# Ten stages of a float32r transformer kernel: the moving halves at ten offsets instead of one

## The reference, cut to what matters

```python
def swiglu(h, w_gate_up, w_down):
    gate, up = jnp.split(h @ w_gate_up, 2, axis=-1)
    return (jax.nn.silu(gate) * up) @ w_down
```

## Time and profile before

| what | value |
|---|---|
| median of 2 runs | 1613.93 us (1613.84 to 1614.02) |
| the profiled execution | 1613.48 us |
| its span, first to last instruction | 1611.7 us |
| PE busy | 1577.5 us, 98% |
| PEld busy | 1418.1 us, 88% |
| DVE busy | 991.0 us, 61% |
| ACT busy | 825.9 us, 51% |
| mean granted TensorE clock | 0.995 |

### The profile page before, as it was taken

How to read it: one execution, slowest core, us unless ns; L and a number is a source line. 1 busy time by engine, 2 the same in 40 slices (tenths; PEclk the granted TensorE clock), 3 DMA queues, 4 the chain that set the end, 5 groups by cost and what they waited for, 6 DMA issues and landing times.

```text
span 1611.7 us, 25494 instructions
## 1 busy us (share of the span) xinstructions
PE 1577.5 (98%) x10721; PEld 1418.1 (88%) x10721; DVE 991.0 (61%) x1661; ACT 825.9 (51%) x1191; POOL 153.2 (10%) x141
## 2 busy tenths in 40 slices
PE   7999999999999999999999999999999999989997
PEld 6878899987889989998899999889888888879986
DVE  6786744445645575556665667668747776665554
ACT  4565543444569755444454465444544546354442
POOL 2220010100002200111001100001000000001100
PEclk9999999999999999999999999999999999999999
DMA  9757866777663356556555576598572565585552
GB/s 332 249 178 252 274 219 229 246 247 245 237 211 105 111 194 200 190 192 218 192 183 178 189 148 193 182 187 175 135 156 62 143 158 182 167 265 190 195 190 78
DMA packets 224417, 309.40 MB, mean 192 GB/s; under 512 B 5004, under 2 KB 146720, under 8 KB 224304
## 3 DMA queue, kind: packets, MB, share of 16 engines
q1 hardware_dynamic: 222208, 301.48, 61.1%
q0 software_dynamic: 1664, 5.84, 1.0%
q10 hardware_dynamic: 432, 0.45, 0.1%
HBM read 306.71 MB, written 1.05 MB: 191 GB/s over the span
## 4 chain that ended last, share of the span: by engine, by line
PE 86%; DVE 8%; ACT 4%; issue 1%; DMA 1%; POOL 0%; ACTq 0%; DVEq 0%
PE ps L137 84%; PE ps L140 2%; DVE wl L150 2%; DVE SM L160 1%; DVE MT L160 1%; ACT wh L146 1%; ACT L146 1%; ACT SA L146 1%; DVE X L160 0%; ACT SA L147 0%; DMA raw<-in_a_w_qkv_dram 0%; DVE MT L157 0%; DMA X<-in_x_dram 0%; ACT FT L146 0%; DVE SM L157 0%
## 5 line engine op out<-in xcount | busy, mean ns | idle before, releaser
L150 DVE TENSOR_TENSOR wl<-raw,wh 128x1024 fp32r<-128x1024 f32 x498 | 611.6, 1267 | 395.8 <-ACT wh L146 395.1
L146 ACT ACTIVATE wh<-raw 128x1024 fp32r<-128x1024 f32 x498 | 502.0, 1053 | 228.5 <-PE ps L137 109.1
L137 PE MATMUL ps<-XPf,wh 128*128 128x256 f32 x1408 | 243.5, 279 | 0.0
L137 PEld LDWEIGHTS ps<-XPf,wh 128*128 128x128 f32 x1408 | 212.8, 188 | 4.5 <-ACT wh L146 2.5
L137 PE MATMUL ps<-XPf,wl 128*128 128x256 f32 x704 | 195.5, 278 | 0.0
L137 PE MATMUL ps<-XPc,wh 128*128 128x256 f32 x832 | 145.8, 280 | 0.0
L137 PE MATMUL ps<-wh,HTH 128*128 128x512 f32 x352 | 137.6, 391 | 0.0
L137 PE MATMUL ps<-wl,HTH 128*128 128x512 f32 x352 | 137.2, 390 | 0.0
L137 PE MATMUL ps<-wh,HTL 128*128 128x512 f32 x352 | 137.2, 390 | 0.0
L137 PEld LDWEIGHTS ps<-XPf,wl 128*128 128x128 f32 x704 | 132.9, 189 | 0.0
L137 PEld LDWEIGHTS ps<-XPc,wh 128*128 128x128 f32 x832 | 126.1, 188 | 1.8 <-ACT wh L146 0.8
(11 more groups left out here) (348 smaller groups left out, 2741.0 us busy)
## 6 DMA issues: line engine op xcount, KB each, us to landing
raw<-in_w_ffn_in_dram SPq DMA_DIRECT2D x66, 1024.0 KB, 5.1
raw<-in_ffn_w_gate_up_dram SPq DMA_DIRECT2D x44, 1024.0 KB, 5.1
raw<-in_w_in_dram SPq DMA_DIRECT2D x40, 1024.0 KB, 8.4
raw<-in_w_ada_dram SPq DMA_DIRECT2D x36, 1024.0 KB, 6.0
raw<-in_w_ffn_out_dram SPq DMA_DIRECT2D x30, 1024.0 KB, 5.1
raw<-in_ffn_w_down_dram SPq DMA_DIRECT2D x20, 1024.0 KB, 5.1
raw<-in_a_w_qkv_dram SPq DMA_DIRECT2D x12, 1024.0 KB, 7.4
raw<-in_kv_w_dram SPq DMA_DIRECT2D x8, 1024.0 KB, 5.7
```

Source lines behind the costliest of these rows:

```text
L137: return NOTHING if self.e is None else self.e.matmul(o, l, r, start=start, stop=stop, skip_group_check=skip)
L146: return self.e.activation(o, i, fn, bias=bias, scale=scale)
L150: return NOTHING if self.e is None else self.e.tensor_tensor(o, a, b, f)
```

## The change

The tiles get offsets of their own, one for each stage, all multiples of 4 bytes and most of them no multiple of 32. Since the allocator is given multiples of 32, a tile is allocated 8 elements longer and a view of it begins up to 7 elements further on. No instruction is added, removed or moved; shapes, order and waits stay the same. The tiles that are stationary operands alone keep 0 or 256.

```diff
-        MAIN_AT = dict(h0=192, ha=0, f0=192, hk=192, hq=192, ho=0, f1=192, e=192, hm=192, hh=0, l=192)
-        CTX_AT = dict(c1=192, c2=192, hb=256, hw=256)
-        XP = {n: at("XP" + n, [P, 2, 8, T], xt0 + d, F32R) for n, d in MAIN_AT.items()}
+        MAIN_AT = dict(h0=188, ha=0, f0=208, hk=204, hq=204, ho=0, f1=216, e=200, hm=196, hh=0, l=184)
+        CTX_AT = dict(c1=208, c2=200, hb=256, hw=256)
+
+        def halves_at(n, off):
+            t = at("XP" + n, [P, 16 * T + 8], off // 32 * 32, F32R)
+            w = off % 32 // 4
+            return t[:, w:w + 16 * T].rearrange("p (h k t) -> p h k t", h=2, k=8)
+
+        XP = {n: halves_at(n, xt0 + d) for n, d in MAIN_AT.items()}
...
-        XP.update({n: at("XP" + n, [P, 2, 8, T], c_.o + d, F32R) for n, d in CTX_AT.items()})
+        XP.update({n: halves_at(n, c_.o + d) for n, d in CTX_AT.items()})
```

## The result

The changed kernel takes 1645.98 us (1645.72 to 1646.24) against 1613.93: a ratio of 1.0199, 95% interval 1.0182 to 1.0215. I had forecast 1608.4 and a range up to 1621. Its profiled execution has a span of 1643.9 us, 32.2 us more than before.

The account below looks back on a forecast made before the run. TensorE's matmul pace was taken to bound the kernel. Moving reads gave -5.5 us, the other terms 0: 1613.5 us became 1608.0, and 0.45 us for the median made 1608.4; range 1603 to 1621 us, about 8 in 10.

Parts of the forecast that it names:

- What bounds the kernel: Whole kernel: TensorE busy for 1577.5 of 1611.7 us at full clock, so the matmuls' pace makes the time.
- the price of the moving reads: Matmuls on moving halves: between 8.3 us won and 20.8 us lost; two thirds of the gain taken, -5.5 us.
- The two modes: Matmuls at offset 192: median 277 ns, pace 113.6 ns (short mode), or 282 ns, pace 118.0 ns (long mode).
- The halves as weights: 864 matmuls with h0, hk, hm and c2 as stationary operands: 0 taken, ends -1.8 and +1.8 us.
- All long: Rival: the new offsets hold the 118.0 ns pace in every stage, 20.8 us lost, 1634.7 us; chance 0.03.
- The hint of the better side: Stationary halves: offset cost gone at 0, 2.1 ns at 192, so moving tiles from 192 towards 256 should gain.
- Odd starts: Moving reads starting off multiples of 32 or 16 bytes: 0 taken, upper end 2 ns a matmul, 13.2 us.
- Writes and waits: DVE's writes of the halves and PE's waits: 0 taken, no wait added; about 1 us if writes were 10% slower.
- That the offset does not matter and the stages draw their mode anew: Rival: offset does not select the stages' pace; 1611 to 1617 us, 1614 in the middle; chance 0.22.
- Costlier starts: Rival: each moving read beginning off a boundary takes one more fetch; 1623 and 1627 us; chance 0.20 for 1617 to 1627.
- Half rate at odd words: Rival: stages at 4 modulo 8 (h0, hk, hq, hm) run at half pace, 131 us more, 1745 us; chance 0.04.
- a third mode: Matmul pace that no row of the kernel before shows; named as what would make the prediction wrong, without size or chance.

Follow-up runs that it names:

- run 13: Changed kernel with every moving tile at 208, a multiple of 16, weights as before: 1642.42 us.
- runs 11 and 12: Changed kernel with weights 4 bytes on and moving tiles at 196, and with weights 8 bytes on and moving tiles at 200: 1669.75 and 1664.01 us.

## Why the prediction was wrong

**What bounds the kernel: right.** The time is the matmuls' pace, the other engines did the same work in the same busy time, and a change without an instruction acted through that pace alone.

**The failed step: the price of the moving reads.** I let it lie "between two ends", all short mode and all long mode, 113.6 and 118.0 ns, and took -5.5 us; it measured +32.2 us. That the paces of the trace at 192 bound those at other offsets was assumed; the trace of before holds one offset for these tiles and could not show it. The two modes are not the ends: the stages of the changed kernel run at 118.6 to 121.7 ns, all above the long mode. The mean step of the moving reads went from 114.7 ns, the mix of the two modes, to 119.8. Added up from start to start over both traces, the matmuls on the moving halves take 32.2 us more and the halves as weights 3.9 us more; everything else takes 3.8 us less, 2.8 us of it PE's shorter idle time. That is the span's growth of 32.2 us but for rounding. "All long", which I priced at 20.8 us and gave 0.03, was the nearest in size. Which paces an offset gives is measured; why is open.

**The hint of the better side: wrong.** Going from 192 towards 256 was to get cheaper, since 0 costs nothing where the halves are stationary. At 208, 224 and 240 the step is 119.1, 118.3 and 117.2 ns, and at 0 it is 119.9: the hint did not carry over from one form to the other. Nor did it hold in its own: h0, hk, hm and c2 as stationary operands take about 232 ns at 208 (run 13), against 229 at 192.

**The halves as weights: taken as 0, measured at about 3.5 us** (576 x 4.1, 96 x 6.5, 96 x 3.8 and 96 x 1.4 ns from the steps in hm, hk, h0 and c2; 3.9 us with the gaps between them). The bound of 1.8 us was too narrow for the same reason.

**Odd starts: taken as 0, worth 3.6 us here (run 13).** My bound of 13.2 us held this time. But the earlier trace rows were no fair witness. From start to start all three of their products, odd heads or not, take 216 to 217 ns for 257 columns within a group, 0.84 ns a column against 0.44 for float32r: they bear no extra cost at a pace half as fast, and in runs 11 and 12 odd starts of both operands took all that the good distance gives.

**Writes and waits: right,** the writes within 2 ns, the waits 0.6 us shorter.

**The rivals.** That the offset does not matter and the stages draw their mode anew fell with the result: no stage kept either pace, and 1646 us lies far above 1617. Costlier starts had the right sign and named f1 and l as the stages that could only lose, and they lost most (7.6 and 7.7 us); but its mechanism, which needs starts off a line, is the smaller part, and 1623 to 1627 us was too low. Half rate at odd words did not occur: hm at 196 has 121.7 ns. The text ahead of the result named the case that came true, a third mode, and gave it no chance and no price.

## What to carry to other kernels

With a fresh weight load for each float32r matmul, the distance between weights and moving operand modulo 256 bytes was worth 3 to 6% of the step here, so it is worth a sweep: in multiples of 16 bytes, for each form of product by itself. If one operand must move, move the other along by the same multiple of 16 bytes and measure (a shift of 16 kept the pace, shifts of 4 and 8 did not). Over the whole kernel the best placement found gained 0.5%. Bounds read from a trace that holds one value of a parameter are bounds for that value alone; a change to values that no row shows needs a chance for a regime outside them. Compare starts, not durations: 282 ns stood for 118 ns in one kernel and for 120 in another.

## What the runs showed of the hardware that I had not expected

- Two offsets of the fifteen multiples of 16 that I tried are good with the weights at 0: 192 and 112. Every other one costs 4 to 7 ns in 113 as a stage's mean. Why these two, 80 bytes apart, is open.
- At 192 with the weights at 0 a call runs at one of two paces, about 113.4 or 117.8 ns; f1 and l kept the lower one throughout, while f0 changed between pieces of five calls and e between single calls. 64 shows the same two. With both operands moved on by 16 bytes, or at 112, no call ran at 117.8.
- With weights as the moving operand, distance 0 gives 227 ns at starts of 0 and 230 at starts of 16; distance 192 gives 229 with the weights at 0 and 227 with the weights at 16.
- With one load of three moved off the good distance the mean step is nearly that of all three moved (117.8 against 118.7 ns), but the long mode alone has 117.8 too. What in the read path does this, no run here shows.
